# Turned squares stored column by column for DMA and strided TensorE weights, and the sparse mixture one place earlier on VectorE, in a two-layer hybrid attention trunk

## What is computed

```python
h = rms_norm(x, pre_w, NORM_EPS)
proj = jnp.einsum('bsd,dn->bsn', h, w_in)          # 1024 -> 4680 columns
dq, dk, dv, dg, sq, sk, sv, sg, iq, ik, iw = jnp.split(proj, SPLIT_OFFSETS, axis=-1)
# group A: 4 heads, two maps of 64 dims each, attn = p[:, :, 0] - lam * p[:, :, 1]
oa = diff_attention(rope(dq), rope(dk), dv, lam)
oa = rms_norm(oa, subln_w, SUBLN_EPS) * (1.0 - lambda_init) * jax.nn.silu(dg)
# group B: 4 heads of 128 dims; each query keeps the 64 keys of highest index score
logits = jnp.einsum('bqhd,bkd->bqhk', rope(iq), rope(layer_norm(ik)))
score = jnp.einsum('bqhk,bqh->bqk', jax.nn.relu(logits), wi)
_, idx = lax.top_k(causal(score), n_sel)
p = jax.nn.softmax(causal_and_selected(q @ k.T * scale)); ob = (p @ v) * jax.nn.silu(sg)
y = jnp.einsum('bsm,md->bsd', jnp.concatenate([oa, ob], -1), w_out)
return x + rms_norm(y, post_w, NORM_EPS)
```

## Time and profile before

| what | before |
|---|---|
| median of 3 runs (lowest, highest) | 303.1 us (302.99, 303.43) |
| the profiled execution | 302.85 us |
| its span, first to last instruction | 301.1 us |
| TensorE, matmuls | 292.4 us busy, 97% |
| VectorE | 234.9 us, 78% |
| ScalarE | 163.9 us, 54% |
| GpSimd | 67.6 us, 22% |
| mean granted TensorE clock | 0.996 |
| moved by DMA | 60.01 MB in 62229 packets |

### The profile page before, as it was taken

How to read it: one execution, slowest core, us unless ns; L and a number is a source line. 1 busy time by engine, 2 the same in 40 slices (tenths; PEclk the granted TensorE clock), 3 DMA queues, 4 the chain that set the end, 5 groups by cost and what they waited for, 6 DMA issues and landing times.

```text
span 301.1 us, 4401 instructions
## 1 busy us (share of the span) xinstructions
PE 292.4 (97%) x1568; PEld 246.4 (82%) x1568; DVE 234.9 (78%) x474; ACT 163.9 (54%) x284; POOL 67.6 (22%) x116
## 2 busy tenths in 40 slices
PE   8999999999999999999999999999999999999992
PEld 7799777788787888788888988778878788887892
DVE  4752989899999997955984786878999999787343
ACT  5986963736577473603665855473737747390101
POOL 6558210303030220101060740012303030210101
PEclk9999999999999999999999999999999999999998
DMA  7999959457518569860059799937653675742011
GB/s 242 370 371 386 371 214 354 135 143 227 195 69 210 209 211 303 191 201 23 0 158 369 242 350 250 325 108 204 209 150 131 146 272 152 202 70 72 0 70 70
DMA packets 62229, 60.01 MB, mean 199 GB/s; under 512 B 34560, under 2 KB 39424, under 8 KB 62208
## 3 DMA queue, kind: packets, MB, share of 16 engines
q1 hardware_dynamic: 61920, 59.47, 62.8%
q10 hardware_dynamic: 288, 0.26, 0.3%
HBM read 54.48 MB, written 5.24 MB: 198 GB/s over the span
## 4 chain that ended last, share of the span: by engine, by line
PE 40%; DVE 37%; ACT 8%; DMA 6%; POOL 4%; issue 3%; SPq 1%; POOLq 0%; DVEq 0%; ACTq 0%
DVE w_lo L987 14%; PE bank_a L470 8%; PE bank_a L461 7%; PE bank_a L466 7%; PE bank_s L618 6%; DMA w_raw<-in_w_in 6%; PE bank_a L618 5%; ACT xt_pbuf L831 4%; DVE work L1107 4%; DVE xt_pbuf L1124 3%; DVE top L1106 3%; DVE xt_pbuf L1140 3%; DVE mixn L1150 2%; DVE mixn L1036 2%; PE bank_s L559 1%
## 5 line engine op out<-in xcount | busy, mean ns | idle before, releaser
L987 DVE TENSOR_TENSOR w_lo<-w_raw,w_hi 128x2048 fp32r<-128x2048 f32 (+1 forms) x46 | 98.8, 2154 | 18.5 <-ACT w_hi L763 18.3
L763 ACT ACTIVATE w_hi<-w_raw 128x2048 fp32r<-128x2048 f32 (+1 forms) x46 | 81.9, 1784 | 31.9 <-PE bank_a L470 23.4
L461 PE MATMUL bank_a<-w_hi,h_hi 128*128 128x512 f32 (+1 forms) x272 | 72.5, 388 | 0.0
L470 PE MATMUL bank_a<-w_lo,h_hi 128*128 128x512 f32 (+1 forms) x272 | 70.0, 379 | 0.5 <-DVE w_lo L987 0.5
L466 PE MATMUL bank_a<-w_hi,h_lo 128*128 128x512 f32 (+1 forms) x272 | 69.9, 379 | 0.0
L470 PEld LDWEIGHTS bank_a<-w_lo,h_hi 128*128 128x128 f32 x272 | 49.7, 188 | 10.5 <-DVE w_lo L987 1.0
L466 PEld LDWEIGHTS bank_a<-w_hi,h_lo 128*128 128x128 f32 x272 | 49.8, 188 | 9.8
L461 PEld LDWEIGHTS bank_a<-w_hi,h_hi 128*128 128x128 f32 x272 | 47.9, 188 | 10.4 <-issue 2.7
L831 ACT ACTIVATE xt_pbuf<-xt_pbuf,st 128x128 f32<-128x128 f32 (+1 forms) x48 | 21.3, 444 | 25.1 <-DVE st L1124 25.1
L1417 POOL TENSOR_TENSOR rt<-nat,tab 128x256 f32<-128x256 f32 x10 | 7.4, 741 | 112.5 <-ACT nat L815 112.5
L815 ACT ACTIVATE nat<-bank_a,st 128x512 f32<-128x512 f32 x20 | 13.5, 681 | 19.6 <-PE bank_a L470 19.6
(11 more groups left out here) (196 smaller groups left out, 431.1 us busy)
## 6 DMA issues: line engine op xcount, KB each, us to landing
w_raw<-in_w_in SPq DMA_DIRECT2D x30, 1024.0 KB, 6.0
w_raw<-in_w_out SPq DMA_DIRECT2D x8, 1024.0 KB, 6.1
w_raw<-in_w_in SPq DMA_DIRECT2D x8, 584.0 KB, 7.3
turned<-mixn SPq DMA_DIRECT2D x20, 128.0 KB, 2.7
prm<-in_rows SPq DMA_DIRECT2D x2, 705.0 KB, 7.0
w_raw<-in_w_in SPq DMA_DIRECT2D x2, 512.0 KB, 6.3
xres<-in_x SPq DMA_DIRECT2D x2, 512.0 KB, 9.5
dqT<-turned SPq DMA_DIRECT2D x2, 512.0 KB, 5.9
```

The costliest lines, as they stand in the source:

```text
L461: pe.matmul(bank, h_hi[:, HALF * half + kk, tok], whi[:, kk, :], start=half == 0 and kk == 0, stop=False)
L470: mm = pe.matmul(bank, h_hi[:, HALF * half + kk, tok], wlo[:, kk, :], start=False, stop=half == 1 and kk == HALF - 1)
L763: act.activation(unit(w_hi, u), unit(raw, u), ACT.Copy).then_inc(hi_done.sem, 1)
L987: dve.tensor_tensor(unit(w_lo, u), unit(raw, u), unit(w_hi, u).bitcast(F32), ALU.subtract).then_inc(lo_done.sem, 1)
```

## The change

The squares are kept in another order. VectorE writes element c of square-column j of slot s (a slot is one block and head) to place (j, c, s) of the partition, with the slot as innermost index: neighbouring elements of a slot are 8 elements apart (4 for PS0). So the row that `put` moves for one square-row is one run of 256 elements instead of eight of 32, and for PS0 one of 128 instead of four. `get` moves rows of the same length as before. The buffers keep this order, and TensorE reads its weights with a step of 8 (or 4) elements (`gathered`). The layer-0 copy into `iqT` writes with the same step, and TensorE's transposes before it are sorted by block instead of by head. Apart from this, `gate_dsa(0)` moves ahead of `drain_mix(T_MD1)` on VectorE. No instruction is added or removed on any engine.

```diff
@@ -138,12 +138,12 @@
         v_dsa = sb("v_dsa", [P, BLOCKS, WIDTH])
         ikn = sb("ikn", [P, BLOCKS, IDX_DIM + IDX_HEADS])
         ik2 = sb("ik2", [P, BLOCKS, 2, IDX_DIM])
-        iqT = sb("iqT", [P, BLOCKS, HEADS, P])
+        iqT = sb("iqT", [P, BLOCKS * HEADS * P])
         ikT = sb("ikT", [P, SEQ])
-        dqT = sb("dqT", [P, BLOCKS, HEADS, P])
+        dqT = sb("dqT", [P, BLOCKS * HEADS * P])
         dkT = sb("dkT", [P, HEADS, SEQ])
-        sqT = sb("sqT", [P, BLOCKS, HEADS, P])
-        skT = iqT[:, :, :, :].rearrange("p b f t -> p (b f t)").rearrange("p (f s) -> p f s", f=HEADS)
+        sqT = sb("sqT", [P, BLOCKS * HEADS * P])
+        skT = iqT[:, :].rearrange("p (f s) -> p f s", f=HEADS)
         xt = sb("xt_pbuf", [P, XT_N])
         pbuf = xt[:, PRE_N:XT_N].rearrange("p (a n) -> p a n", n=WIDTH)
         pT = sb("pT", [P, 3, WIDTH])
@@ -173,7 +173,7 @@
         subln = st[:, 152:153]
         rd, rs = st[:, 154:156], st[:, 156:158]
         squares = mixn[:, :, :].rearrange("p b n -> p (b n)")
-        prob_buf = {PS0: dkT[:, 0:2, :].rearrange("p f t -> p (f t)"), PS1: dqT[:, :, :, :].rearrange("p b f t -> p (b f t)")}
+        prob_buf = {PS0: dkT[:, 0:2, :].rearrange("p f t -> p (f t)"), PS1: dqT[:, :]}
 
 
         A = [pb("bank_a0", [P, WIDTH]), pb("bank_a1", [P, WIDTH])]
@@ -306,6 +306,13 @@
 
         y_w = pbuf[:, :, :].rearrange("p (b a) n -> p b (a n)", b=BLOCKS)
         ik_tmp = pbuf[:, 1, 0:2 * BLOCKS * 2 * HD].rearrange("p (t b d) -> p t b d", t=2, b=BLOCKS)
+        def gathered(buf, s, parts=slice(0, P), slots=BLOCKS * HEADS):
+
+            return buf[parts, :].rearrange("p (t s) -> p s t", s=slots)[:, s, :]
+
+        def by_column(buf):
+            return buf.rearrange("p (j c s) -> p s j c", j=SQUARES, c=LANES)
+
         block = ctx.enter_context(nc.Block())
 
 
@@ -315,8 +322,8 @@
 
             def put(n, buf, written):
                 for i in range(SQUARES):
-                    to = scratch[n].rearrange("(j r) a (i c) -> i r a j c", j=SQUARES, i=SQUARES)[i]
-                    sp.dma_start(to, buf[i * LANES:(i + 1) * LANES, :].rearrange("r (a j c) -> r a j c", j=SQUARES, c=LANES)).then_inc(written, 16)
+                    to = scratch[n].rearrange("(j r) i m -> i r j m", j=SQUARES)[i]
+                    sp.dma_start(to, buf[i * LANES:(i + 1) * LANES, :].rearrange("r (j m) -> r j m", j=SQUARES)).then_inc(written, 16)
 
             def put_probs(layer, n):
                 sp.wait_ge(prob_squares.sem, prob_squares.at(layer, n - PS0 + 1))
@@ -327,10 +334,10 @@
 
                 sp.wait_ge(o_filled.sem, o_filled.at(layer, 1 if n == PS0 else 2))
                 dst = pT[:, 0, :] if n == PS0 else pT[:, 1:3, :].rearrange("p s n -> p (s n)")
-                sp.dma_start(dst, scratch[n].rearrange("p a t -> p (a t)")).then_inc(prob_landed[n].sem, 16)
+                sp.dma_start(dst, scratch[n].rearrange("p i m -> p (i m)")).then_inc(prob_landed[n].sem, 16)
 
             def get(n, dst, landed):
-                sp.dma_start(dst[:, :, :, :].rearrange("p b f t -> p (b f) t"), scratch[n]).then_inc(landed, 16)
+                sp.dma_start(dst[:, :], scratch[n].rearrange("p i m -> p (i m)")).then_inc(landed, 16)
 
             def turned(i):
                 sp.dma_start(xt[:, cuts[i]:cuts[i + 1]], x_t[:, cuts[i]:cuts[i + 1]]).then_inc(xt_landed[i], 16)
@@ -556,7 +563,7 @@
                     for i, pair in enumerate(pairs):
                         for odd in range(2):
                             rows_h = slice(IDX_DIM * odd, IDX_DIM * (odd + 1))
-                            mm = pe.matmul(banks[odd][:, i * n:(i + 1) * n], iqT[rows_h, b, pair, :],
+                            mm = pe.matmul(banks[odd][:, i * n:(i + 1) * n], gathered(iqT, b * HEADS + pair, rows_h),
                                            ikT[rows_h, 0:n], start=True, stop=True)
                             if i == len(pairs) - 1:
                                 mm.then_inc(s_filled.sem, 1)
@@ -568,7 +575,7 @@
                     for i, h in enumerate(heads):
                         for m in range(2):
                             rows_m = slice(DIFF_QK * m, DIFF_QK * (m + 1))
-                            mm = pe.matmul(banks[m][:, i * n:(i + 1) * n], dqT[rows_m, b, h, :],
+                            mm = pe.matmul(banks[m][:, i * n:(i + 1) * n], gathered(dqT, b * HEADS + h, rows_m),
                                            dkT[rows_m, h, 0:n], start=True, stop=True)
                             if i == len(heads) - 1:
                                 mm.then_inc(s_filled.sem, 1)
@@ -576,7 +583,7 @@
                 def dsa_scores(j, b, heads):
                     bank, n = bank_s(j), P * (b + 1)
                     for i, h in enumerate(heads):
-                        mm = pe.matmul(bank[:, i * n:(i + 1) * n], sqT[:, b, h, :],
+                        mm = pe.matmul(bank[:, i * n:(i + 1) * n], gathered(sqT, b * HEADS + h),
                                        skT[:, h, 0:n], start=True, stop=True)
                     mm.then_inc(s_filled.sem, 1)
 
@@ -638,9 +645,8 @@
                     pe.wait_ge(proj_moved.sem, proj_moved.at(layer, 4))
                     pe.wait_ge(rope_done.sem, rope_done.at(layer, 1))
                     for n in range(2):
-                        for i in range(4):
-                            f, b = 2 * n + i // 2, i % 2
-                            mm = pe.transpose(S[n][:, i * P:(i + 1) * P], nat[:, 0, b, f * P:(f + 1) * P], ident[:, :])
+                        for f in range(HEADS):
+                            mm = pe.transpose(S[n][:, f * P:(f + 1) * P], nat[:, 0, n, f * P:(f + 1) * P], ident[:, :])
                         mm.then_inc(iq_filled, 1)
                 first(7)
                 second(7)
@@ -712,7 +718,7 @@
                 turn_mix(T_MD1, 1, 1)
 
                 pe.wait_ge(prob_landed[PS0].sem, prob_landed[PS0].at(layer, 16))
-                values(2, 0, v_dsa, [[slot(0, h)] for h in range(HEADS)], place(layer, SV, 0) + 1)
+                values(2, 0, v_dsa, [[gathered(pT[:, 0, :], h, slots=HEADS)] for h in range(HEADS)], place(layer, SV, 0) + 1)
 
                 pe.wait_ge(t_drained.sem, t_drained.at(layer, T_MD0 + 1))
                 out_part(0, 0, 0)
@@ -725,7 +731,7 @@
                 out_part(1, 0, 0)
 
                 pe.wait_ge(prob_landed[PS1].sem, prob_landed[PS1].at(layer, 16))
-                values(3, 1, v_dsa, [[slot(1 + h // 2, 2 * (h % 2) + t) for t in range(2)] for h in range(HEADS)],
+                values(3, 1, v_dsa, [[gathered(pT[:, 1:3, :].rearrange("p s n -> p (s n)"), 2 * h + t) for t in range(2)] for h in range(HEADS)],
                        place(layer, SV, 1) + 1)
                 out_part(1, 0, 1).then_inc(y_done.sem, 1)
 
@@ -1033,12 +1039,12 @@
                 def turn_squares(slot, rope, done):
 
                     dve.wait_ge(rope_done.sem, rope_done.at(layer, rope))
-                    dve.transpose(squares, nat[:, slot, :, :].rearrange("p b n -> p (b n)")).then_inc(done, 1)
+                    dve.transpose(by_column(squares), nat[:, slot, :, :].rearrange("p b (f j c) -> p (b f) j c", j=SQUARES, c=LANES)).then_inc(done, 1)
 
                 def turn_probs(n, use):
                     dve.wait_ge(exps_done.sem, exps_done.at(layer, use + 1 - S_DIFF0))
                     probs = pbuf[:, 0, :] if n == PS0 else pbuf[:, 1:3, :].rearrange("p s n -> p (s n)")
-                    dve.transpose(prob_buf[n], probs).then_inc(prob_squares.sem, 1)
+                    dve.transpose(by_column(prob_buf[n]), probs.rearrange("p (s j c) -> p s j c", j=SQUARES, c=LANES)).then_inc(prob_squares.sem, 1)
 
                 def drain_mix(j, dst_hi, dst_lo, b, weight=None):
                     dve.wait_ge(t_filled.sem, t_filled.at(layer, j + 1))
@@ -1206,8 +1212,8 @@
                 if layer == 0:
                     for n in range(2):
                         dve.wait_ge(iq_filled, n + 1)
-                        dve.tensor_copy(iqT[:, :, 2 * n:2 * n + 2, :].rearrange("p b f t -> p f b t"),
-                                        S[n][:, :].rearrange("p (f b t) -> p f b t", f=2, b=BLOCKS)).then_inc(iq_copied, 1)
+                        to = iqT[:, :].rearrange("p (t s) -> p s t", s=BLOCKS * HEADS)[:, HEADS * n:HEADS * (n + 1), :]
+                        dve.tensor_copy(to, S[n][:, :].rearrange("p (s t) -> p s t", s=HEADS)).then_inc(iq_copied, 1)
                 split_lo(layer, 9)
                 drain(T_IK, ikT[:, :])
                 split_lo(layer, 10)
@@ -1282,8 +1288,8 @@
                 gate_diff(1)
                 split_lo(layer, 22)
 
+                gate_dsa(0)
                 drain_mix(T_MD1, m_hi, m_lo, 1, subln)
-                gate_dsa(0)
                 drain_mix(T_MS0, h_hi, h_lo, 0)
                 split_lo(layer, 23)
                 gate_dsa(1)
@@ -1502,7 +1508,7 @@
     nc = bacc.Bacc("TRN2", target_bir_lowering=False, num_devices=1)
```

(2 more changed lines are left out.)

## The result

| | before | after |
|---|---|---|
| median | 303.05 us | 315.47 us |
| lowest to highest | 302.99 to 303.43 | 314.94 to 316.12 |
| ratio after/before | | 1.0408, 95% interval 1.0385 to 1.0431 |
| profiled execution, span | 302.85, 301.1 us | 314.94, 313.1 us |

The account below looks back on a forecast made before the run. TensorE's own stream, busy 97% of the span, was taken to bound the kernel. 302.85 - 1.38 for part 1, everything else at zero, gave 301.47, plus 0.25 for the median: 301.7 us; range 300.9 to 307.8.

Parts of the forecast that it names:

- Part 1: VectorE's gate_dsa(0) ahead of draining T_MD1: both TensorE waits before T_MS0 vanish, 1.38 us; TensorE arrives at 127.72.
- The DMAs: Longer put runs: packets fall from 62229 to about 34070, puts land sooner, no time gained.
- TensorE's weights: Strided weight loads on TensorE: bounded between zero and 10 us in all, taken at zero.
- the upper end: TensorE's strided weight loads needing twice their time: 5.0 us a layer, 10 us in all.
- half-row loads: diff_scores and index_logits, 128 columns on half the rows: a doubled pair takes 0.208 us, 1.4 us a layer.
- the groups with 256 columns: TensorE's 256-column records: the matmul, about twice as long, covers even a doubled load.
- the full-row records: values on v_dsa and dsa_scores, 128 columns: doubled loads set the pace at 0.222 us, 3.55 us a layer.
- rival 1: TensorE's 128-column strided weight loads at half pace: 311.7 us, slower beyond 11 ns extra a load; chance 0.19.
- VectorE's transposes: VectorE's strided writes: between no change and twice as long, taken at zero, staying 1.24 us for 1024 elements.
- Rival 2: Only VectorE's strided writes cost: transposes double, gate_dsa(0) 3.7 us later, gap before T_MS0, 307.7 us; chance 0.09.
- TensorE's own delay covers it: If transposes double along with TensorE's loads, TensorE's delay covers most of theirs; time about rival 1's.

## Why the prediction was wrong

**Part 1** was right in its working: 1.38 us forecast, 1.45 measured alone. In the changed kernel the wait is gone as well, only no longer thanks to VectorE: TensorE arrives at 132.48, 4.8 us after the 127.72 of the prediction, and with the old order it does not wait either.

**The DMAs** were right: 34069 packets for 34070, puts that land in 2.3 us in place of 2.7 and leave the queue sooner (0.44 us of issue in place of 0.69), and no effect on the time that shows: with the old puts and strided weights the kernel takes 315.23 us, with the new ones 315.47.

**TensorE's weights** is the step that failed. The prediction bounded the term at 0 and 10 us and wrote "The nearest rows are the same loads at 0.111, and I take zero". The measured term is 13.8 us. Two things went wrong. First the choice: the rows showed loads with no slack against their matmuls, so the sign turned at 11 ns a record, and the measured extra is about 120. A row of consecutive loads says nothing on strided ones; it was the nearest row and not evidence for the lower end. The rule that spoke against the edit (the Trainium skill, Advanced Engine Details and Errata, SBUF Cachelines: lines of 16 bytes, at least two hits on each) is borne out by this case's runs: step 2, with two hits on a line, is nearly free (0.117 us a load for 0.112), steps 4 and 8 are doubled, and step 3 lies halfway (0.174). It was told and given 0.19. Second the size of the upper end: half-row loads were put at 1.4 us a layer and measured 2.04 (a pair of records went from 0.124 to 0.251 us, not from 0.119 to 0.208); the groups with 256 columns were said to cover a doubled load and cost 0.97 us a layer, `dsa_scores` there coming down to the load's own pace (8 in 1.90 us) and the half-row groups losing 0.2 us each; the full-row records cost 0.12 us each, 3.88 a layer for 3.55. So rival 1 had the right mechanism and place, and its 311.7 us were 3.8 short. The range ended below it.

**VectorE's transposes** were taken at zero too, and that failed as well: they last 1.7 times as long (2.15 us for 1.24). Rival 2, which let them double, had 4.6 us more than the kernel before; with consecutive weights 306.31 - 302.83 = 3.5 us more were measured. Its mechanism was right, its price too high, as the transposes did not double, and its place one turning too late, with smaller waits at other turnings that it did not have. That TensorE's own delay covers it when both happen was right (315.23 against 315.47 us). The layer-0 copy into `iqT`, which writes with the step too, was given no term. Each of its two halves went from 0.68 to 1.15 us, and TensorE waits 0.23 us for VectorE there:

```profile
L1216 DVE COPY iqT<-bank_s x2: 1127/1148/1169, 40.2 to 41.2; 128x512 f32<-128x512 f32 x2
...
44.84 2.17 PE L566 MATMUL bank_s<-ikT,iqT 64*128 64x128 f32 x16 [0.23 <-DVE ikT L1030]
```

## What to carry to other kernels

Before a layout is changed for the DMA's sake, ask who reads it on the engine that bounds the program: 28000 packets less were worth nothing that could be seen here, and a step of 16 or 32 bytes on 208 weight loads a run cost 4%. On float32 TensorE's weight loads at a step of two elements were nearly free, at three half again as long and at four doubled, so interleave by two at most; where the trace has no row for an access pattern, measure that one instruction before choosing between the bounds. A small gain (the order on VectorE) that is bundled with such a change cannot be seen in the sum and has to be run alone.

## What the runs showed of the hardware

A strided access cost about the same on every side that was tried: TensorE's weight loads (0.225 to 0.233 us for 128 elements at step 4, before 0.112), its moving operand ((1.98 - 0.405)/7 = 0.225 us for a record at step 4), VectorE's reads (2.12 us for 1024 elements at step 8, before 1.24) and VectorE's writes (2.15 us at step 8, 2.02 at step 4). For TensorE's weights it goes by the 16-byte pieces touched, 1.76 to 1.83 ns each, from step 2 to step 4, and hardly grows beyond. In the kernel with the strided moving operand, eight and sixteen records stand thus in the timeline:

```profile
126.47 1.98 PE L595 MATMUL bank_o<-v_dsa,pT 128*128 128x128 f32 x8
...
136.94 3.79 PE L595 MATMUL bank_o<-v_dsa,pT 128*128 128x128 f32 x16
```

The sixteen give (3.79 - 0.405)/15 = 0.226 us, against 0.225 for weight loads in the same group: both operands pay alike. What stays open: why a weight load of the eight-record group comes out some 4% dearer than one of the sixteen, whether VectorE also goes by pieces of 16 bytes (step 3 was not tried on it; writes at step 2 left the transposes at 1.24 us, and reads at step 2 were not tried), and why its writes at step 8 take 6% longer than at step 4.
